# Forty-eight projection chunks: two of their three products in one wide matmul

## The reference

```python
def first_block(...):
    for l in range(2):
        h = modulate(rms_norm(x, g_mix[l]), sa, ca)          # and the same for ctx
        ...                                                  # differential attention and pooling
        x = x + ga * (mix @ w_out[l])
        x = x + gm * (square(relu(modulate(rms_norm(x, g_mlp[l]), sm, cm) @ w_mlp1[l])) @ w_mlp2[l])
        ...                                                  # ctx the same, in layer 0 only
    return rms_norm(x, g_final)

def second_block(x, ...):
    for l in range(2):
        hn = rms_norm_2(h, mix_norm_g[l])
        mix = even_mixer(hn, ...) if l == 0 else odd_mixer(hn, ...)   # each ends in  @ w_out
        h = h + mix
        h = h + conv_ffn(rms_norm_2(h, ffn_norm_g[l]), ...)           # (u * gelu(g)) @ w_down
    return rms_norm_2(h, final_norm_g)
```

## Time and profile before

| | |
|---|---|
| three runs, us | 1743.23, 1744.52, 1744.61 |
| profiled execution, us | 1742.86 |
| its span in the profile, us | 1741.1 |
| mean granted TensorE clock | 0.949 of full speed |
| VectorE busy | 1063.5 us (61%) |
| ScalarE busy | 738.8 us (42%) |
| GpSimd busy | 98.3 us (6%) |
| read from HBM | 255.95 MB |

### The profile page before, as it was taken

One profiled execution on the slowest core, in us unless ns is written; L12 is line 12 of the kernel. 1 busy time (PEld: TensorE's weight loads), 2 busy tenths in 40 slices (PEclk: granted clock), 3 DMA queues, 4 the chain that ended last, 5 costly groups with the idle time before them and its releaser, 6 DMA issues.

```text
span 1741.1 us, 27219 instructions
## 1 busy us (share of the span) xinstructions
PE 1607.3 (92%) x11292; PEld 1437.4 (83%) x11292; DVE 1063.5 (61%) x1539; ACT 738.8 (42%) x1053; POOL 98.3 (6%) x95
## 2 busy tenths in 40 slices
PE   5899888999999997997999989768999998899997
PEld 2688566777777776977999988768999998899997
DVE  1743836433333336665655677676877876887875
ACT  2212733313232233254544444424654656665553
POOL 0000000000000000000000020000210201020110
PEclk7899988999999998999999989959999999899998
DMA  9564021534443432222445534403455444454551
GB/s 402 211 245 170 14 84 50 193 134 156 169 145 145 169 120 97 100 95 73 146 171 190 193 111 146 145 1 122 170 193 185 179 146 145 146 186 178 179 186 48
DMA packets 35580, 258.34 MB, mean 148 GB/s; under 512 B 3968, under 2 KB 3984, under 8 KB 4512
## 3 DMA queue, kind: packets, MB, share of 16 engines
q1 hardware_dynamic: 28944, 211.12, 33.2%
q0 software_dynamic: 6544, 45.90, 7.1%
HBM read 255.95 MB, written 1.05 MB: 148 GB/s over the span
## 4 chain that ended last, share of the span: by engine, by line
PE 79%; DVE 13%; ACT 4%; issue 2%; DMA 1%; SPq 0%; DVEq 0%; ACTq 0%
PE ps L436 17%; PE ps L437 17%; PE ps L438 17%; PE ps L456 4%; PE ps L457 4%; PE ps L458 4%; PE ps L523 2%; DVE w_lo L1280 2%; PE ps L507 2%; PE ps L509 2%; PE ps L508 2%; DMA ada_g<-in_w_ada 1%; PE ps L543 1%; DVE small L1402 1%; ACT w_hi L887 1%
## 5 line engine op out<-in xcount | busy, mean ns | idle before, releaser
L887 ACT ACTIVATE w_hi<-w_raw 128x1024 fp32r<-128x1024 f32 x380 | 397.7, 1055 | 618.7 <-PE ps L438 389.9
L1280 DVE TENSOR_TENSOR w_lo<-w_raw,w_hi 128x1024 fp32r<-128x1024 f32 x380 | 468.4, 1237 | 255.5 <-ACT w_hi L887 252.5
L436 PE MATMUL ps<-h_hi,w_hi 128*128 128x256 f32 (+1 forms) x1712 | 542.6, 317 | 27.9 <-DVE h_lo L1331 13.5
L437 PE MATMUL ps<-h_lo,w_hi 128*128 128x256 f32 (+1 forms) x1712 | 536.3, 313 | 0.0
L438 PE MATMUL ps<-h_hi,w_lo 128*128 128x256 f32 (+1 forms) x1712 | 535.5, 313 | 0.0
L436 PEld LDWEIGHTS ps<-h_hi,w_hi 128*128 128x128 f32 x1712 | 332.7, 194 | 58.9 <-issue 23.6
L438 PEld LDWEIGHTS ps<-h_hi,w_lo 128*128 128x128 f32 x1712 | 332.5, 194 | 17.7
L437 PEld LDWEIGHTS ps<-h_lo,w_hi 128*128 128x128 f32 x1712 | 333.1, 195 | 16.7 <-issue 0.2
L436 PE MATMUL ps<-g_hi,w_hi 128*128 128x256 f32 (+1 forms) x448 | 141.4, 316 | 0.0
L456 PE MATMUL ps<-g_hi,w_hi 128*128 128x256 f32 (+1 forms) x448 | 140.9, 314 | 0.0
L437 PE MATMUL ps<-g_lo,w_hi 128*128 128x256 f32 (+1 forms) x448 | 140.6, 314 | 0.0
(11 more groups left out here) (287 smaller groups left out, 2137.5 us busy)
## 6 DMA issues: line engine op xcount, KB each, us to landing
w_raw<-in_w_stream SPq DMA_DIRECT2D x190, 1024.0 KB, 4.8
ada_r<-in_w_ada POOLq DMA_DIRECT2D x24, 1024.0 KB, 5.1
ada_g<-in_w_ada POOLq DMA_DIRECT2D x16, 1024.0 KB, 6.8
ada_r<-in_w_ada SPq DMA_DIRECT2D x4, 1024.0 KB, 10.1
ada_g<-in_w_ada SPq DMA_DIRECT2D x4, 1024.0 KB, 22.9
x<-in_x_in SPq DMA_DIRECT2D x1, 2048.0 KB, 17.4
pmat<-in_pool_mats POOLq DMA_DIRECT2D x2, 1024.0 KB, 6.4
out<-y_out SPq DMA_DIRECT2D x1, 1024.0 KB, 3.9
```

The source lines that it names most:

```text
L436: mm(o, wh, hi[:, k, cols], start=(k == 0), stop=False)
L437: mm(o, wh, lo[:, k, cols], start=False, stop=False)
L887: A(w_hi[:, n % 2, k, :].rearrange("p k n -> p (k n)"), w_raw[:, n % 4, k.start * CH:k.stop * CH], ACT.Copy)\
L1280: TT(w_lo[:, n % 2, k, :].rearrange("p k n -> p (k n)"), w_raw[:, n % 4, k.start * CH:k.stop * CH], w_hi[:, n % 2, k, :].rearrange("p k n ...
```

## The change

In the 48 chunks the high weight meets the high and the low part of the input in one matmul of 512 columns: h_hi and h_lo become the two halves of one tensor h_two (g_two and xr_two likewise), and the moving operand is [128, 2, 256] with the halves 16 KB apart (8 KB in xr_two). The accumulator's bank then holds hi*hi + lo_w*hi in its first half and hi*lo in its second. The low weight's product remains a matmul of 256 columns. For each k and m there are 2 matmuls and 2 weight loads instead of 3; the columns streamed are the same. At k = 7 the narrow matmul comes first and the wide one last. `gemm_wide` and `gemm_wide_pair` are otherwise `gemm_f` and `gemm_f_pair`.

VectorE adds the first half of the banks to x, waits for that (`own.step`, `own.join`), and adds the second half. In the loop over the MLP's quarters the join's value is computed from the loop's index. Chunks that don't add to the residual, and the first block's layer 0, keep their three matmuls.

```diff
-        h_hi = place("h_hi", [P, KT, ALLT], F32R)
-        h_lo = place("h_lo", [P, KT, ALLT], F32R)
+        h_two = place("h_two", [P, 2, KT, ALLT], F32R)
+        h_hi, h_lo = h_two[:, 0, :, :], h_two[:, 1, :, :]
         g_base = top[0]
-        g_hi = place("g_hi", [P, KT, ALLT], F32R)
-        g_lo = place("g_lo", [P, KT, ALLT], F32R)
+        g_two = place("g_two", [P, 2, KT, ALLT], F32R)
+        g_hi, g_lo = g_two[:, 0, :, :], g_two[:, 1, :, :]
...
+            def products(o, wh, wl, two, k, cols):
+                o2 = o.rearrange("p (c t) -> p c t", c=2)
+                if k == KT - 1:
+                    mm(o[:, 0:SEQ], wl, two[:, 0, k, cols], start=False, stop=False)
+                    return mm(o2, wh, two[:, :, k, cols], start=False, stop=True)
+                mm(o2, wh, two[:, :, k, cols], start=(k == 0), stop=False)
+                return mm(o[:, 0:SEQ], wl, two[:, 0, k, cols], start=False, stop=False)
+            def gemm_wide(n, two, cols, ready, at=same):
+                start_chunk(n, at)
+                s = n % 2
+                for k in range(KT):
+                    if k == KT // 2:
+                        pe.wait_ge(lo_ready, at(n + 1))
+                    if ready is not None:
+                        pe.wait_ge(ready[0], at_of(ready, at)(k + 1))
+                    for m in range(2):
+                        wh, wl = w_hi[:, s, k, m * P:(m + 1) * P], w_lo[:, s, k, m * P:(m + 1) * P]
+                        last = products(ps[:, 2 * s + m, :], wh, wl, two, k, cols)
+                    if k == KT // 2 - 1:
+                        last.then_inc(half_used, 1)
+                last.then_inc(gemm_done, 1)
...
+            def gemm_wide_pair(n, two, cols, ready, at=same, early=KT - 2, middle=None):
+                def part(n, ks):
+                    s = n % 2
+                    for k in ks:
+                        if k == KT // 2:
+                            pe.wait_ge(lo_ready, at(n + 1))
+                        if ready is not None:
+                            pe.wait_ge(ready[0], at_of(ready, at)(k + 1))
+                        for m in range(2):
+                            wh, wl = w_hi[:, s, k, m * P:(m + 1) * P], w_lo[:, s, k, m * P:(m + 1) * P]
+                            last = products(ps[:, 2 * s + m, :], wh, wl, two, k, cols)
+                        if k == KT // 2 - 1:
+                            last.then_inc(half_used, 1)
+                    return last
+                for c in range(2):
+                    start_chunk(n + c, at)
+                    part(n + c, range(early))
+                if middle is not None:
+                    middle()
+                for c in range(2):
+                    part(n + c, range(early, KT)).then_inc(gemm_done, 1)
...
+                        elif l and c == 4:
+                            gemm_wide_pair(n, g_two, width, (g_ready, G0["mlp1"], 8, it), at)
+                        elif l and c > 5:
+                            gemm_wide(n, g_two, width, None, at)
...
-            gemm_f_pair(N_EVOUT, h_hi, h_lo, slice(SEQ, ALLT), None, early=KT // 2, middle=gla_outputs)
+            gemm_wide_pair(N_EVOUT, h_two, slice(SEQ, ALLT), None, early=KT // 2, middle=gla_outputs)
             for c in (2, 3):
-                gemm_f(N_EVOUT + c, h_hi, h_lo, slice(SEQ, ALLT), None)
+                gemm_wide(N_EVOUT + c, h_two, slice(SEQ, ALLT), None)
...
             def gated(n, tile0, l, part, at=same):
                 dve.wait_ge(gemm_done, at(n + 1))
-                for m in range(2):
-                    for s in range(2 - l):
-                        c = slice(s * SEQ, (s + 1) * SEQ)
-                        t = tile0 + m
-                        last = STT(x[:, t, c], ps[:, tile0 % 4 + m, c], ada[:, l, part + t, s:s + 1], x[:, t, c],
-                                   ALU.mult, ALU.add)
+                wide = l == 1 and part == 40
+                for half in range(2 if wide else 1):
+                    for m in range(2):
+                        for s in range(2 - l):
+                            c = slice(s * SEQ, (s + 1) * SEQ)
+                            t = tile0 + m
+                            src = ps[:, tile0 % 4 + m, c if half == 0 else slice(SEQ, ALLT)]
+                            last = STT(x[:, t, c], src, ada[:, l, part + t, s:s + 1], x[:, t, c], ALU.mult, ALU.add)
+                            if wide and half == 0:
+                                own.step(last)
+                    if wide and half == 0:
+                        own.join()
                 last.then_inc(psum_free, 1)
             def added(n, tile0, at=same):
                 dve.wait_ge(gemm_done, at(n + 1))
                 t = slice(tile0, tile0 + 2)
-                TT(x[:, t, 0:SEQ], ps[:, 2 * (n % 2):2 * (n % 2) + 2, 0:SEQ], x[:, t, 0:SEQ], ALU.add).then_inc(psum_free, 1)
+                src = ps[:, 2 * (n % 2):2 * (n % 2) + 2, :]
+                own.step(TT(x[:, t, 0:SEQ], src[:, :, 0:SEQ], x[:, t, 0:SEQ], ALU.add))
+                own.join()
+                TT(x[:, t, 0:SEQ], src[:, :, SEQ:ALLT], x[:, t, 0:SEQ], ALU.add).then_inc(psum_free, 1)
...
                 with dve.Fori(0, 3) as it:
+                    if l:
+                        own.enter(it, 8)
                     quarter(it, 0)
+                if l:
+                    own.leave(3)
```

More of the change, by code:

```diff
@@ L201, in build_program @@
         gmask = place("gmask", [P, 8, P], I32, at=a_base)
-        xr_hi = place("xr_hi", [P, KT, SEQ], F32R, at=g_base)
-        xr_lo = place("xr_lo", [P, KT, SEQ], F32R, at=g_base + 8 * KB)
+        xr_two = place("xr_two", [P, 2, KT, SEQ], F32R, at=g_base)
+        xr_hi, xr_lo = xr_two[:, 0, :, :], xr_two[:, 1, :, :]
         rg_a = place("rg_a", [P, KT, SEQ], at=g_base + 16 * KB)
@@ L699, in _ @@
                             ada_next(c)
+                        elif l and c == 4:
+                            gemm_wide_pair(n, g_two, width, (g_ready, G0["mlp1"], 8, it), at)
+                        elif l and c > 5:
+                            gemm_wide(n, g_two, width, None, at)
                         elif c == 4:
-                            gemm_f_pair(n, g_hi, g_lo, width, (g_ready, G0[f"mlp{l}"], 8, it), at)
+                            gemm_f_pair(n, g_hi, g_lo, width, (g_ready, G0["mlp0"], 8, it), at)
                             ada_next(4)
@@ L826, in ffn @@
                         elif c == 8:
-                            gemm_f_pair(n, g_hi, g_lo, slice(0, SEQ), (g_ready, G0[f"ffn{l}"] + 8 * third))
+                            gemm_wide_pair(n, g_two, slice(0, SEQ), (g_ready, G0[f"ffn{l}"] + 8 * third))
                         elif c > 9:
-                            gemm_f(n, g_hi, g_lo, slice(0, SEQ), None)
+                            gemm_wide(n, g_two, slice(0, SEQ), None)
             ffn(0)
@@ L860, in _ @@
             pe.wait_ge(sig_i, 2)
-            gemm_f_pair(N_ODOUT, xr_hi, xr_lo, slice(0, SEQ), (rg_ylo, 0), early=KT // 2)
+            gemm_wide_pair(N_ODOUT, xr_two, slice(0, SEQ), (rg_ylo, 0), early=KT // 2)
             for c in (2, 3):
-                gemm_f(N_ODOUT + c, xr_hi, xr_lo, slice(0, SEQ), None)
+                gemm_wide(N_ODOUT + c, xr_two, slice(0, SEQ), None)
             ffn(1)
```

## The result

The changed kernel takes 1756.52 us (median of 4 runs, 1754.75 to 1759.03), the kernel before 1743.88 on the same chip (4 runs, 1742.74 to 1744.61): ratio 1.0073, 95% interval 1.0059 to 1.0087. It is 12.6 us slower where +6.7 was forecast. The profiled span grew from 1741.1 to 1753.0 us, at nearly the same mean clock (0.949 before, 0.947 after).

The account below looks back on a forecast made before the run. TensorE was taken to bound the middle of stages, VectorE their ends. Saved 7.6 us, added 4.1 (pairs) and 10.2 (ends): net +6.7, forecast 1751.2 us, its own range 1748.5 to 1754, overall 1745.5 to 1757.5.

Parts of the forecast that it names:

- What bounds: Whole kernel: TensorE bounds the middle of a stage, VectorE its end; the change moves work from the first to the second.
- the overall range: Total time: 1745.5 to 1757.5 us, around the forecast of 1751.2 us.
- the clock drops: Rival: new TensorE waits at norms bring half-clock stretches, 4 to 6 us on top, 1756 us; chance 0.12.
- What one removed matmul is worth: Changed chunks: 0.0133 us per removed matmul at full clock, 0.213 us a chunk, at most 10.2 us for 48.
- all 512-column rows sit at 0.2267: TensorE's stream: a wide matmul takes 0.2267 us, so one wide and one narrow take 0.3467 instead of 0.3600.
- The pairs: Behind chunk pairs TensorE newly waits for banks: 0.78 us three times in the MLP, 0.35 five times in FFNs.
- The large ends: Stage ends before both mixers: second additions cost 3.7 us at the MLP's end and 3.0 at ffn0's.
- The output projections and the kernel's end: Even and odd output ends cost 1.4 us each, savings included; ffn1's last addition costs 0.7 us.
- Additions stay covered: Rival: VectorE's additions stay hidden and all full-clock savings count, -7.9 us, 1736.6; chance 0.05.
- The ends absorb most: Rival: ends absorb most, pairs at half price, output stages at 0: net +1 to +3 us; chance 0.13.
- The wide matmul saves nothing: Rival: reading two places costs what the removed instruction saved, +14 us, 1758.5; chance 0.10.

Follow-up runs that it names:

- with and without the cover: Changed kernel with 17 end chunks as before, pairs split one k earlier (FFN) or two (MLP): 1738.44 us; the same without the earlier split: 1743.88 us.
- the kernel with three narrow matmuls: Changed kernel, but the wide matmul is two narrow ones into two half banks, both halves still added by VectorE: 1760.6 us, ratio 1.0092.
- the first experiment: Changed kernel, but VectorE adds only the first half of each bank, leaving out part of the result: 1739.76 us, ratio 0.9975.
- the order two and two: Changed kernel with 17 end chunks as before, pairs split earlier, and matmuls ordered wide, wide, narrow, narrow: 1737.38 us, ratio 0.9968.

## Why the prediction was right, and where its size was off

**What bounds.** Right. The change moves work to the engine that bounds the ends, and 17 chunks at the ends carry all the loss.

**The number.** 1756.5 lies inside the overall range, but outside the forecast's own 1748.5 to 1754. It is close to the 1756 of the rival "the clock drops", and part of the distance is that rival's mechanism.

**What one removed matmul is worth: mis-sized.** The step "all 512-column rows sit at 0.2267", hence 0.3467 for a couple, was read from streams of one width. Alternating, a couple takes 0.3467 in some stretches and 0.3531 in others, and 64 removed matmuls save 0.56 to 0.60 us where nothing waits, not 0.85. Eight groups at 0.27 less are 2.1 us of the miss. The Trainium skill ("TensorE: Matmul & The Clock Gate", Back-to-back issue gap) has, for an isolated matmul, 2.5 ns over the columns; an estimate by it is 0.16 us saved for a group. The runs, at 0.56 to 0.73, lie nearer to the row's 0.85 than to that.

**The pairs.** Right in place and mechanism, to the row: forecast 0.78, found 0.73; forecast 0.35, found 0.35. Taken with and without the cover, a pair costs 0.85 and 0.45 us: 0.07 more is the slow start behind the wait, the rest was not traced. That is another 0.7 us of the miss.

**The large ends.** The trace has `gated` at +0.92 as forecast and `added` at +0.73 against 0.71. The MLP's end fits (+3.6 against +3.7), and so does ffn0's (+3.3 against +3.0) within what that stretch varies by. The wait for squares before the even mixer was forecast at about 8 us and is 5.87: the sums start as late as forecast, but TensorE arrives late too, at 1026.03 - 5.87 = 1020.16 against 1022.35 - 4.38 = 1017.97. In the last quarter it waits 0.57 and 0.29 us for banks, and 0.83 more for which the profile names no releaser.

**The output projections and the kernel's end: mis-sized.** They were charged with VectorE's delay alone. The waits are there (0.95 and 0.98 us), but behind each TensorE drops to 1.2 GHz, and the rival "the clock drops", counted at 0.12, came true in part. Of the 1.6 us that the stretch from sums to broadcast grows by, about 1.0 is the clock: with the same additions and the clock full, the odd output costs +1.3 and the kernel's end +0.7, near the forecast, in the kernel with three narrow matmuls. At the kernel's end the sums start 0.21 apart instead of 0.11, 1.1 us in all. Three such places hold 3.3 us of the miss, 1.1 each. The end of ffn0 has the longest stretch at half clock, 6.8 us, but its delay can't be told from the forecast's. That the drops come with the waits is shown; what decides whether a wait is followed by one is open, so part of the 3.3 us could have come out otherwise.

**The sum.** 2.1 + 0.7 (groups and pairs) + 3.3 (three drops) + 0.2 (the two large ends) + 0.2 (ffn1's last third) = 6.5, less 1.1 in the two stretches that differ from execution to execution: 5.4. The spans differ from the forecast by 1753.0 - 1747.8 = 5.2. That these two stretches came out short is luck, and it made the miss look smaller.

**The rivals.** "Additions stay covered" falls by the changed kernel, though it holds for 31 chunks once the pairs are split earlier. "The ends absorb most" falls: the two large ends absorbed 0.2 us at most, and of the 2.2 us of three additions inside an output projection about 1.0 was absorbed, which the forecast had counted. "The wide matmul saves nothing" falls by the first experiment.

## What to carry to other kernels

A trade of TensorE's time for VectorE's is priced per place: in the middle of a stage it costs nothing if TensorE has enough matmuls to do before it asks for the bank again; at a stage's last chunk every operation is on the path. Make the trade chunk by chunk, keep the old form at the ends, and move the point where the next chunk asks for the bank; here that turned +12.6 into -5.4 us, and -6.5 with the order two and two. And where a wait is put ahead of TensorE's stream, count a half-clock stretch behind it as a risk with a price of its own: here it came behind ten of the ten waits of 0.93 to 0.99 us and cost about 1 us each.

## What the runs showed of the hardware

- A matmul of 512 columns and one of 256 in turn take 0.3467 or 0.3531 us for both, depending on the stretch; two and two 0.348; each alone 0.2267 and 0.1200. What decides between the two was not found; the distance of the operand's halves (2 or 16 KB) does not.
- At three norms in thirteen traces, waits before the sums of 0.55, of 0.93 to 0.99 and of 1.83 to 2.01 us were followed by 3.4 to 6.8 us at the half clock, in all sixteen cases; waits of 0.07, 0.12, 0.54, 1.09 and 1.59 left the clock full, and so did the eighteen cases without a wait.
- The first matmul behind a wait for `x` starts 0.14 us after VectorE's operation ends (865.16 after 863.23 + 1.79), and the second one 0.07 us later than in the stream.
- Two operations of 128x512 on VectorE with a join between them start 0.72 to 0.73 us apart, of 0.69 us each: the join costs 0.03 to 0.04.
